# Attention outputs stored to DRAM between two phases, rings of four value and three key groups, page numbers read once

## The reference, cut to what matters

```
xn = rms(x, norm1_w);  zq, zk, zv, hq, hf, hi, hg = split(xn @ w_in)
o_da = differential attention of 4 heads (prompt: causal; sample: over past_k, past_v and the new rows)
       past_k = cache_k[l][page_table],  past_v = cache_v[l][page_table]
o_hg = HGRN2 recurrence of 4 heads, normed and gated
h = x + concat([o_da, o_hg]) @ w_out
y = h + mixture of experts(rms(h, norm2_w))      # 16 experts, 2 for each token
```

## Time and profile before

| what | value |
|---|---|
| time, median of 3 runs | 1530.07 us (1523.56 to 1531.3) |
| the profiled execution's own time | 1530.65 us |
| its span in the profile | 1528.9 us |
| busy in the span | PE 76%, PEld 57%, DVE 38%, ACT 30%, POOL 16% |
| phases, us from the span's start | up to attention's end 0 to 592.3; heads and decode 592.3 to 948.4; mix 948.4 to 1134; experts 1134 to 1528.9 |
| sample attention's loads | keys 128 and values 128, of 256 KB, median 3.7 and 3.8 us from issue to landing |

### The profile page before, as it was taken

One profiled execution on the slowest core, in us unless ns is written; L12 is line 12 of the kernel. 1 busy time (PEld: TensorE's weight loads), 2 busy tenths in 40 slices (PEclk: granted clock), 3 DMA queues, 4 the chain that ended last, 5 costly groups with the idle time before them and its releaser, 6 DMA issues. The chain is left out here.

```text
span 1528.9 us, 24713 instructions
## 1 busy us (share of the span) xinstructions
PE 1163.0 (76%) x9100; PEld 874.1 (57%) x9100; DVE 581.6 (38%) x1022; ACT 461.0 (30%) x857; POOL 239.3 (16%) x262
## 2 busy tenths in 40 slices
PE   4699998697979794167666757899839989999940
PEld 3699998486868683055444544677624434444410
DVE  5220110363636363466777773311252111121131
ACT  6111100444444454355555554212100100111121
POOL 4100000000000002121222221212011212222231
PEclk9999999698989897578787779899859999999975
DMA  4420310211111114778788774832133898887567
GB/s 120 110 63 22 84 29 25 74 44 57 57 57 57 57 44 129 231 238 268 245 260 265 244 248 146 302 136 97 62 109 96 230 286 262 253 261 204 128 140 185
DMA packets 160578, 226.50 MB, mean 148 GB/s; under 512 B 16081, under 2 KB 104402, under 8 KB 160402
## 3 DMA queue, kind: packets, MB, share of 16 engines
q1 hardware_dynamic: 133826, 168.63, 33.9%
q0 software_dynamic: 12992, 46.93, 12.3%
q10 hardware_dynamic: 13664, 9.64, 2.2%
HBM read 182.17 MB, written 47.45 MB: 150 GB/s over the span
## 5 line engine op out<-in xcount | busy, mean ns | idle before, releaser
L2135 PE MATMUL ps<-ring,e_xgT 128*128 x400 | 182.1, 609 | 8.7 <-SPq L2056 8.7
L2135 PEld LDWEIGHTS ps<-ring,e_xgT 128*128 128x128 f32 x400 | 76.2, 195 | 97.6 <-issue 97.6
L2164 PE MATMUL ps<-ring,e_hT 128*128 x200 | 92.4, 605 | 16.9 <-ACT e_hT L2193 16.9
L629 PE MATMUL ps<-xh,a_wh 128*128 128x384 f32 (+1 forms) x288 | 101.4, 352 | 0.0
L629 PE MATMUL ps<-xl,a_wh 128*128 128x384 f32 (+1 forms) x288 | 97.3, 338 | 0.0
L629 PE MATMUL ps<-xh,a_wl 128*128 128x384 f32 (+1 forms) x288 | 97.0, 337 | 0.0
L2087 POOL DMA_INDIRECT y_rows<-e_oE,slot_to x32 | 50.5, 1579 | 276.6 <-issue 224.8
L2188 ACT ACTIVATE e_sg<-ps 128x256 f32<-128x256 f32 x32 | 12.3, 383 | 256.2 <-PE ps L2135 243.6
L1559 DVE STREAM_TRANSPOSE d_KT<-d_K 128x2048 f32<-128x2048 f32 x32 | 73.7, 2304 | 23.3 <-DMA d_K<-in_cache_k 23.2
L1087 POOL TENSOR_TENSOR h_X<-h_X,h_q 128x256 f32<-128x256 f32 (+1 forms) x56 | 45.9, 830 | 232.6 <-ACT h_X L1344 117.2
L501 DVE COPY p_vs<-ps 128x256 f32<-128x256 f32 (+1 forms) x36 | 15.3, 424 | 173.5 <-PE ps L449 173.5
(11 more groups left out here) (342 smaller groups left out, 2476.2 us busy)
## 6 DMA issues: line engine op xcount, KB each, us to landing
d_K<-in_cache_k SPq DMA_DIRECT2D x128, 256.0 KB, 3.7
d_V<-in_cache_v SPq DMA_DIRECT2D x128, 256.0 KB, 3.8
ring<-in_w_gate SPq DMA_DIRECT2D x16, 1024.0 KB, 7.8
ring<-in_w_up SPq DMA_DIRECT2D x16, 1024.0 KB, 12.0
ring<-in_w_down SPq DMA_DIRECT2D x16, 1024.0 KB, 13.8
zT<-a_zs POOLq DMA_DIRECT2D x12, 544.0 KB, 3.0
a_w<-in_w_in SPq DMA_DIRECT2D x12, 512.0 KB, 3.8
y_rows<-ring SPq DMA_DIRECT2D x10, 512.0 KB, 2.6
```

The costliest lines, as they stand in the source:

```text
L629: ins = pe.matmul(m.ps[:, 7, 0:w0], left[:, n % 2, k, :], right[:, k, c0:c0 + w0], start=(k == 0 and j == 0), stop=(k == KD - 1 and j == 2))
L2135: ins = pe.matmul(m.ps[:, 2 + u, :], xgT[:, u, k, :], up_k[:, bass.ds(r * KD + k, 1), :].squeeze(1), start=(k == 0), stop=(k == KD - 1))
L2164: ins = pe.matmul(m.ps[:, 6 + b, :], hT[:, u, f * 128:f * 128 + 128], down_w[:, bass.ds(r * FC + f, 1), b * 512:b * 512 + 512].squeeze(1), ...
```

## The change

Three things are changed.

- `mixT` is split up. `mixH` (128 x 4 x 1088) holds what slots 4 to 7 held. `mixA` (the same size) holds slots 0 to 3 and lives only until attention's end; POOL stores each head's 512 KB of it to DRAM (`mix_rows`) when DVE has written the head's output, and waits for all four stores before the phase ends. The mix phase loads it back into `m_mixA` with two transfers that ACT issues first (columns 0 to 255, 512 KB, and 256 to 1023, 1.5 MB). The sample tokens' outputs stay in SBUF, in `mixS`.
- The 16 KB a partition that this leaves free in the decode phase go to one more slot in each ring: KR 2 to 3, VR 3 to 4.
- The page numbers of a group are read once, for its keys; its value loads use the same registers.

`split_mix` has four instructions of half the width for each tile instead of two. TensorE's, DVE's and ACT's lists are the same otherwise.

```diff
-        m.mixT = sb("mixT", [128, KD, TOK])
+        m.mixH = sb("mixH", [128, HEADS, TOK])
+        m.mixS = sb("mixS", [128, HEADS, NS])
+        m.mix_rows = nc.dram_tensor("mix_rows", (HEADS, 128, SEQ), F32, kind="Internal").ap()
...
+                m.mixA = early.enter_context(nc.sbuf_tensor("mixA", [128, HEADS, TOK], F32))
...
                     pool.dma_start(m.zT[n, h, :, :], zs[:, :]).then_inc(m.z_stored, 16)
                     pool.wait_ge(m.z_stored, h * NZ * 16 + n * 16 + 16)
                     pool.sem_inc(z_left, 1)
+                pool.wait_ge(head_done, h + 1 + 1)
+                pool.dma_start(m.mix_rows[h, :, :], m.mixA[:, h, 0:SEQ]).then_inc(m.mix_stored, 16)
+            pool.wait_ge(m.mix_stored, HEADS * 16)
...
-                dve.scalar_tensor_tensor(m.mixT[:, h, 0:SEQ], oT[:, :], m.subw[:, :], ro[:, :],
+                dve.scalar_tensor_tensor(m.mixA[:, h, 0:SEQ], oT[:, :], m.subw[:, :], ro[:, :],
...
-    KR, VR = 2, 3
+    KR, VR = 3, 4
...
+            pages_of = {}
...
             def load_keys(g):
-                pages = page_numbers(g)
+                pages = pages_of[g] = page_numbers(g)
...
             def load_values(g):
-                pages = page_numbers(g)
+                pages = pages_of.pop(g)
...
-                pool.tensor_copy(mh[:, u, :, 0:n], m.mixT[:, :, cols(t)]).then_inc(mix_rounded, 1)
-                pool.wait_ge(mix_rounded, t + 1)
-                pool.tensor_tensor(ml[:, u, :, 0:n], m.mixT[:, :, cols(t)], mh[:, u, :, 0:n], ALU.subtract).then_inc(mix_split, 1)
+                o, g = mixA[:, :, cols(t)] if t < NT else m.mixS[:, :, :], m.mixH[:, :, cols(t)]
+                ho, hg = mh[:, u, 0:HEADS, 0:n], mh[:, u, HEADS:KD, 0:n]
+                pool.tensor_copy(hg, g).then_inc(mix_rounded, 1)
+                if t in (0, 2):
+                    pool.wait_ge(mix_in[t // 2], 16)
+                pool.tensor_copy(ho, o).then_inc(mix_rounded, 1)
+                pool.wait_ge(mix_rounded, 2 * t + 2)
+                pool.tensor_tensor(ml[:, u, HEADS:KD, 0:n], g, hg, ALU.subtract).then_inc(mix_split, 1)
+                pool.tensor_tensor(ml[:, u, 0:HEADS, 0:n], o, ho, ALU.subtract).then_inc(mix_split, 1)
...
+            for i, c in enumerate((slice(0, 256), slice(256, SEQ))):
+                act.dma_start(mixA[:, :, c], m.mix_rows[:, :, c].rearrange("h p n -> p h n")).then_inc(mix_in[i], 16)
             load_ln_exp(nc, act)
```

More of the change, by code:

```diff
@@ L121, in build @@
         m.ps = ctx.enter_context(nc.psum_tensor("ps", [128, 8, 512], F32))
-        m.z_stored, m.v_stored = (ctx.enter_context(nc.semaphore(n)) for n in ("z_stored", "v_stored"))
+        m.z_stored, m.v_stored, m.mix_stored = (ctx.enter_context(nc.semaphore(n)) for n in ("z_stored", "v_stored", "mix_stored"))
         with ExitStack() as middle:
@@ L470, in read @@
                 for g, (c0, w0) in enumerate(GROUPS):
-                    dst = m.mixT[:, bass.ds(t + HEADS * n, 1), c0:c0 + w0].squeeze(1)
+                    dst = (m.mixA, m.mixH)[n][:, bass.ds(t, 1), c0:c0 + w0].squeeze(1)
                     ins = act.activation(dst, m.ps[:, 3 * n + g, 0:w0], ACT.Copy)
@@ L685, in squares @@
                 for n, s in enumerate((sq, sk)):
-                    z = m.mixT[:, bass.ds(h + HEADS * n, 1), :].squeeze(1)
+                    z = (m.mixA, m.mixH)[n][:, bass.ds(h, 1), :].squeeze(1)
                     act.activation(s[:, :], z, ACT.Square).then_inc(squared[n], 1)
@@ L761, in prepare @@
             def prepare(h):
-                zq, zk = (m.mixT[:, bass.ds(h + HEADS * n, 1), :].squeeze(1) for n in range(2))
+                zq, zk = (mix[:, bass.ds(h, 1), :].squeeze(1) for mix in (m.mixA, m.mixH))
                 dve.wait_ge(r_ready[0], h + 1)
@@ L949, in gate_of @@
         def gate_of(n):
-            return m.mixT[:, n // 2 + HEADS, n % 2 * W:n % 2 * W + wide(n)]
+            return m.mixH[:, n // 2, n % 2 * W:n % 2 * W + wide(n)]
         def unit_cols(t):
@@ L1657, in _ @@
             ro = P[:, HEADS * NS:2 * HEADS * NS].rearrange("p (h t) -> p h t", h=HEADS)
-            dve.scalar_tensor_tensor(m.mixT[:, 0:HEADS, SEQ:TOK], m.kS[:, :, :], m.subw[:, :], ro, ALU.mult, ALU.mult)
+            dve.scalar_tensor_tensor(m.mixS[:, :, :], m.kS[:, :, :], m.subw[:, :], ro, ALU.mult, ALU.mult)
 def mix_phase(nc, a, m):
@@ L1707, in mix_phase @@
         gate = sem("m_gate")
+        mixA, mix_in = sb("m_mixA", [128, HEADS, SEQ]), [sem("m_mix_in0"), sem("m_mix_in1")]
         w_rounded, w_split, mix_rounded, mix_split = (sem(f"m_{n}") for n in (
@@ L1814, in project @@
                     if b == 0:
-                        pe.wait_ge(mix_split, t + 1)
+                        pe.wait_ge(mix_split, 2 * t + 2)
                     if t >= 2:
```

## The result

The changed kernel takes **1512.32 us** (median of 4 runs, 1503.93 to 1513.07) against 1529.25 for the kernel before, a ratio of 0.988 (95% interval 0.985 to 0.990): 17 us faster. The forecast was 1505, range 1494 to 1517. Timed once more on another chip the ratio was 0.986 (0.982 to 0.989). The profiled execution took 1513.07, its span 1511.3.

A forecast was written before the change was run, and what follows sets the result against it. No engine was full; chained waits bound the kernel: TensorE's for value groups and turned keys, VectorE's for a key group. 1530.65 - 16.75 - 18.1 + 3.6 + 5.0 = 1504.4, given as 1505 us, range 1494 to 1517.

The forecast's parts named there:

- Value waits, even units: Decode units 2, 4, 6: the fourth value slot shortens TensorE's value waits until `squares(n)` is late: 16.75 us gained.
- Value waits, odd units: Decode's odd units: ScalarE's 13 transfers after its squares set the pace, so 0 gained; other bound 7.3 us gained.
- The first unit: Decode's first unit: key groups load earlier, `cumulate(1)` comes 18.0 us earlier, `keys(1, 2)` 13.0; with another 5.1, 18.1 us gained.
- Steady loads: Decode after the first unit: each load burst ends before the next begins; cost 0, bounds 0 and 10 us.
- Attention's end: End of the attention phase: it waits for POOL's store of the last head; 3.6 us lost, between 3.0 and 6.
- The mix phase: Mix phase's start: loading 2.1 MB again while `w_out` comes in costs 5.0 us, bounds 2 and 13.5.
- the dear bound of 13.5: Mix phase's start: if `w_out` has half the rate until 2.1 MB are through, the reload costs 13.5 us.
- Rival F: Decode becomes bound by the loads, deciding from 1.24 us a load: slower, 1539 there, 1575 at 1.4; chance 0.05.
- D: Decode: key groups land late at each burst's start, 1.5 us in each of 7 units, +10.5, 1515; chance 0.10.
- E: Decode: the fourth value group still lands late, only the first unit gains; 1521, or 1526; chance 0.06.
- C: Mix phase's start dearer, as four staging slots pass the delay on chunk by chunk: +8.5, 1513; chance 0.12.
- A: The whole kernel: the forecast itself, with all its terms, 1498 to 1512; chance 0.55.

The follow-up runs named there:

- Experiment 6: The changed kernel with SP instead of ScalarE issuing the odd units' 13 transfers, behind its value loads and after `output(n)`: 1489.13 us, ratio 0.972.
- experiment 4: The changed kernel with page numbers read a second time for the values: 1505.78 us; timed again 1508.61, beside 1508.41 for the changed kernel on the same chip.
- experiment 5: The changed kernel with page numbers read once in the first two units, then a second time for the values from the third unit on: 1504.97 us, ratio 0.983.

## Why the prediction was right, and where not

The direction, the range and the mechanism of the gain were right. The point was 7 us too low, for the most part by one term, and 1512.3 lies just outside the forecast's own narrower range of 1498 to 1512.

- *Value waits, even units*: -16.75 forecast, -16.4 measured. That `squares(n)` is late next was read rightly: TensorE starts units 3, 5 and 7 at most 0.15 us after the squares end.
- *Value waits, odd units*: 0 forecast, +7.9 measured. **This is the step that failed.** I had seen that ScalarE's issuing sets the odd units, and bounded the term by 0 and a gain; a loss was not among the bounds, for I took the 6.67 us of unit 3 as a fixed duration. The same 13 took 6.67 to 12.08 us in the traces of these kernels. Experiment 6 shows that ScalarE's time for issuing held the odd units; why that time grew is not settled. Some of it probably comes from an edit that I costed at nothing: the page reads saved "lie in SP's slack", but where their pauses are kept ScalarE's transfers were shorter (experiments 4 and 5). The value waits that I took for the upper bound are also misread: the three odd ones are 2.51, 3.65 and 2.77 us, 8.9 and not 7.3, since the four even ones are not all 8.86.
- *The first unit*: -18.1 forecast, -20.7 measured. The 0.95 us a load was taken from rows in which two page reads of 1.55 us stood within each twelve loads. I took off one page read for the values where four fall away; experiment 4 puts them back and moves unit 1's start by 4.8 us. SP was through with the first 28 loads 49.7 us after its first transfer, where I had 57.0; VectorE then waited for the fifth group, not the seventh, and `keys(1, 2)` and the squares came 15.6 us earlier, not 13.0. The other 5.1 and the 18.0 of `cumulate(1)` came as forecast. (The 652.3 for the seventh group lets it land 3.0 us after its issue, where the table's median is 3.7.) The earlier start of unit 1 is within the bounds that I gave, and without these 2.6 us the time would have been further off: in part the errors cancel.
- *Steady loads*: 0 forecast, and right: no key wait in any later unit, and the DMA share of the steady part is 0.80, not the 0.86 I expected.
- *Attention's end*: +3.6 forecast, +5.1 measured, within 3 to 6. The landing was right, 2.9 us where I had 3.0, but it counts from the start of the issue, so the 0.53 for the issue was added twice. Missing were GpSimd's 0.72 us before the issue, where I had 0.1, and the 1.8 us from the landing to the next phase, where I had only the 0.27 of before.
- *The mix phase*: +5.0 forecast, +4.4 in this pair of traces and 4.9 over all. Bytes gave the right size, though not at the 317 GB/s I had: from 926.44 to the last rounding at 946.66 it was 351, against 314 before (948.40 to 965.00). ScalarE waits 3.38 and 3.34 us for the second and fourth chunk of `w_out`, nowhere over 2.1 before, and by the eighth the loss is 3.8 us, far from the dear bound of 13.5. The Trainium skill, "DMA: Bandwidth & Descriptors", section "Queues, rings and completion order", lets each engine go round between the queue rows a packet at a time, by which the first chunks come later; the trace agrees with that in kind: the fourth chunk is rounded 5.1 us later than before, the last 3.8.
- Together the terms missed by +7.9 (odd units), -2.6, +1.5, -0.6, +0.4, and +2.1 of unit 7 and of the projections, for which no step of mine stands: 8.7 us between the span forecast and that measured. The 0.9 before attention's end comes with no edit there, and that end moved between 589.8 and 593.1 in other traces of the same code.

Rival F fell, since SP's loads took 0.70 us, far from 1.24. D and E fell: no key waits in bursts, no value wait left. C was priced 8.5 over the forecast at the mix phase's start; the time came out near its 1513, but for another cause, as the start cost what A says. The chances for "faster" add to 0.93, not 0.92, which changes nothing.

## What to carry to other kernels

A queue that an engine issues from is part of its critical path. When a profile puts an engine's wait down to "issue", ask which other engine is idle then and could issue: here the move gave 19 us, nearly as much as the change (22 on that chip). But test such a move together with the change that frees the mover: the same edit was worth nothing while SP's own list waited for ring slots.

When a rate is read from a grouped row of a queue, take out what the sequencer does between the transfers, and price an edit by it. And a duration of issuing is not a constant (6.67 to 12.08 us here for the same 13 transfers): give it a bound on both sides.

## What the runs showed of the hardware that was not expected

- One same row of 13 transfers took from 6.67 to 12.08 us to issue by ScalarE, and the last of them (`h_v<-zi`) from 0.53 to 3.66 us, with the DMA engines' share at 0.95 to 1.05 in the six stretches of the two kernels compared; issued by SP ahead of the first unit, at a share of 0.53, the last eleven take 4.4 us.
- A store of one head (512 KB) issued by GpSimd let the next phase begin 4.7 us after its issue began, though it had landed after 2.9; with the halves issued by SP it began 3.1 us after the first one's issue and 0.4 us after the second had landed.
- The mix and experts phase, untouched by the rings, varied by 6 us between traces (580.2 to 586.2), as much as the single effects of most experiments here. Phase lengths and single gaps told apart what whole times could not.
